# Hybrid decoder step: the last quarter of the out-projection as seven block products, and two pieces of expert weights asked for later

## The chip, the cores and the metric

The kernel runs on one core of one Trainium2 chip. The metric is the device time of one execution in microseconds (us). Three runs of the kernel before gave a median of 1177.78 us (1176.58 to 1179.69).

## What is computed

One layer of a decoder for 320 token rows (256 of a prompt, 64 of eight samples), all in float32. What matters here is what comes after attention:

```
h = x + mixed @ w_out                     # (320, 2048) @ (2048, 2048): the out-projection
n = rms_norm(h, g_ffn)
g_logits = n @ w_rg                       # 4 expert groups, top-1
e_logits = n @ w_re                       # 8 experts in that group, top-2
act  = silu(n @ w_gate[e]) * (n @ w_up[e]) * gates[e]
out  = h + sum over e of act @ w_down[e]  # 32 experts, 256 wide each
```

## The kernel before

Each engine has its own instruction list, written out by hand, and semaphores join them. Four stages follow one another: the projection of the memory tokens, nine chunks of 512 columns of the input projection with the attentions woven between them, the out-projection in four chunks of 512 columns, and the experts.

**A chunk of a projection** takes four quarters of the contraction (`q` = 0 to 3, 512 deep each). A quarter's weights are one block of 1 MB, loaded by SP into one of three slots of `wring` (`weights`). For each quarter PE does three units, and each unit raises `unit_done` by one. There are two ways to do the 256 prompt rows. The plain way is `unit` twice, for 128 rows by 512 columns each (line 576). The other is Winograd's form of Strassen's product: the 256 by 512 deep by 512 columns are seen as two by two blocks, and seven block products of 128 by 256 (line 594) replace eight. `plain_products` does the three whose weights are blocks as loaded, `mixed_products` the four whose weights are sums or differences of blocks. DVE makes those four in `wmix` (`mix_weights`, lines 1292 to 1308) and has made the sums of the tokens before, in `y_mix` (`mix_tokens`). When the last quarter is through, ACT copies the first product out of PSUM (`first_product`), and DVE adds the seven together in `fresh` (`add_products`, lines 1319 to 1323, and `add_fourth`, line 1330). The 64 sample rows are a unit of their own in both ways (`small_unit`, line 586). In the kernel before, chunks 0, 1 and 2 of the out-projection go as seven products and chunk 3 the plain way.

**Behind each chunk of the out-projection** come the residual (lines 1630 and 1634 on DVE; line 1643 for chunk 3), the squares for the norm (line 1205 on ACT), the scaling by `g_ffn` (`scale_tile`, line 1613), the transposes of the 320 rows on PE (`turn_n2`, line 922), their copies out of PSUM on ACT (`turned_n2`, line 1211) and the router's products (`route_sums`, line 930). For chunks 0 to 2 PE does `turn_n2` and `route_sums` inside the next chunk. For chunk 3 they come at the end.

**Routing** goes from the router's logits (copied by ACT, line 1226) through PE transposes and some 40 small DVE operations to a one-hot table, the gather of the first block of tokens (`gather`, line 990) and the list of blocks (`blocks_ready`, line 1733). PE does products with the unit matrix between them (`keep_busy`, line 975), whose results nobody reads.

**The experts** run in blocks of up to 32 tokens of one expert. Each block uses three pieces of weights of 2 MB, two of gate and up, one of down. A ring of eight places (`A_R`, `RING`) takes them. SP asks for pieces 0, 1 and 2 during chunk 0 of the out-projection, since their places are free by then. For piece 7 it waits for `blocks_ready`, and from piece 8 on each place is asked for again when PE is through with what was in it (`piece_used`). Place 3 lies on `A_KV`, where `y_mix` is, and places 4 and 5 lie on `wring` and `wmix`.

Of the kernel before, what the change touches and what calls it, by code (L numbers as in the profile page):

```python
# [24 lines left out]
ALU = mybir.AluOpType  # L25
# [4 lines left out]
P = 128  # L30
# [5 lines left out]
ROWS = [(0, 128), (128, 128), (256, 64)]  # L36
# [7 lines left out]
COLS = 512  # L44
QTR = 4
# [8 lines left out]
UNITS_M, UNITS_X = 4 * QTR, NCHUNK * QTR * 3  # L54
# [65 lines left out]
def hybrid_step(nc, x_rows, mem_rows, x_t, mem_t, w_proj, w_o, kc, vc, mkc, mvc, cst_d, gv_d, gffn_d,  # L120
                relb_d, onehot_d, w_gu, w_dn, mst_d, o_y, o_k, o_v, o_va, o_mk, o_mv,
                bias_d, bias_q_d):
    with ExitStack() as ctx:
# [13 lines left out]
        ps = ctx.enter_context(nc.psum_tensor("ps", [P, 8, 512], F32))  # L137
# [46 lines left out]
        yT = area(A_Y, KT, NT)  # L184
# [43 lines left out]
        hres = area(A_H, 3, D)  # L228
# [81 lines left out]
        unit_done, z_ready = sem("unit_done"), sem("z_ready")  # L310
# [21 lines left out]
        x_again, h_ready = sem("x_again"), sem("h_ready")  # L332
# [35 lines left out]
            return v[:, :, 0, 0:HALF], v[:, :, 0, HALF:COLS], v[:, :, 1, 0:HALF], v[:, :, 1, HALF:COLS]  # L368

        def regions(v):  # L370
            r = 6 if v in (0, 11) else 0
            return r, r + 1, r + 2, 14, r + 3, r + 4, r + 5

        block = ctx.enter_context(nc.Block())
# [3 lines left out]
        def _(sp):  # L378
# [82 lines left out]
            for s in range(UNITS_X):  # L461
# [14 lines left out]
                n, i = sample_step(s)  # L476
# [35 lines left out]
            def piece(u, e):  # L512

                if u % 3 < 2:
                    h = KT // 2 * (u % 3)
                    sp.dma_start(gate_up[u % RING], w_gu[e, :, h:h + KT // 2]).then_inc(ring_loaded[u % RING], 16)
                else:
                    sp.dma_start(down[u % RING], w_dn[e]).then_inc(ring_loaded[u % RING], 16)

            for o in range(1, 13):  # L520
                sp.wait_ge(unit_done, UNITS_M + UNITS_X + 3 * (o + 1))
                weights(47 + o)
                if o in (1, 3, 5):
                    piece(o // 2, 0)
                if o == 11:
                    piece(3, 1)
            sp.wait_ge(unit_done, UNITS_M + UNITS_X + 45)
            piece(4, 1)
            sp.wait_ge(unit_done, UNITS_M + UNITS_X + 48)
            piece(5, 1)  # L530
            piece(6, 2)
            sp.wait_ge(blocks_ready, 1)
# [2 lines left out]
            last = sp.value_load(cnt_i[0:1, 0:1], min_val=NEXP // BODY - 1, max_val=NBLK // BODY - 1)  # L535
# [32 lines left out]
        def _(pe):  # L568
            mm, tr = nc.tensor.matmul, nc.tensor.transpose
            def unit(i, bank, t, src, kq, first, final):  # L570

                pe.wait_ge(w_loaded[i % SLOTS_W], w_count(i))
                r0, m = ROWS[t]
                for k in range(K4):
                    kt = kq * K4 + k
                    last = mm(ps[:, bank + t, :], src[:, kt, r0:r0 + m], wring[:, i % SLOTS_W, k, :],  # L576
                              start=first and k == 0, stop=final and k == K4 - 1)
                last.then_inc(unit_done, 1)

            def small_unit(i, bank, col, src, kq, first, final):  # L580

                pe.wait_ge(w_loaded[i % SLOTS_W], w_count(i))
                for k in range(K4):
                    kt = kq * K4 + k
                    for j in range(2):
                        last = mm(ps[64 * j:64 * j + 64, bank, col:col + HALF], src[:, kt, NPROMPT:NT],  # L586
                                  wring[:, i % SLOTS_W, k, HALF * j:HALF * j + HALF],
                                  start=first and k == 0 and bank != 7, stop=final and k == K4 - 1, skip_group_check=bank == 7)
                last.then_inc(unit_done, 1)
# [326 lines left out]
            def turn_n2(ch, t):  # L916

                r0, m = ROWS[t]
                pe.wait_ge(g_ready, 3 * ch + t + 1)
                for k in range(4):  # L920
                    kt = 4 * ch + k
                    last = tr(ps[:, 3 * (ch % 2) + t, k * 128:k * 128 + m], n2[0:m, t, kt * 128:(kt + 1) * 128], ident[0:m, 0:m])
                last.then_inc(n2_tr, 1)
# [9 lines left out]
            def out_chunk(ch):  # L933
                for q in range(QTR):
                    i = 2 * QTR + NCHUNK * QTR + ch * QTR + q
                    kq = (q + 1) % QTR if ch == 0 else q
                    if ch == 0 and q == QTR - 1:
                        pe.wait_ge(gate_y, G)
                    if ch == 0:
                        pe.wait_ge(y_mixed, q + 1)  # L940
                    for t in range(3):
                        if ch < 3 and t == 0:
                            plain_products(i, 10 + ch, yT, kq, y_mix, q == 0, q == QTR - 1)
                        elif ch < 3 and t == 1:
                            mixed_products(i, 10 + ch, yT, kq, y_mix, q == 0, q == QTR - 1)
                        elif ch < 3:
                            small_unit(i, 7, HALF, yT, kq, q == 0, q == QTR - 1)
                        elif t < 2:
                            unit(i, 3, t, yT, kq, q == 0, q == QTR - 1)
                        else:  # L950
                            small_unit(i, 5, 0, yT, kq, q == 0, q == QTR - 1)
                        if ch == 0 and 3 * q + t < G:
                            gate_turn(3 * q + t)
                        if ch == 3 and q == QTR - 1 and t:
                            turn_n2(3, t - 1)
                    if ch and q == 1:
                        for t in range(3):
                            turn_n2(ch - 1, t)
                    if ch and q == 2:
                        route_sums(ch - 1, 0, NT)  # L960
            for ch in range(4):
                out_chunk(ch)
            turn_n2(3, 2)
            route_sums(3, 0, NPROMPT)
            route_sums(3, NPROMPT, NT).then_inc(lgT_mm, 1)
            pe.wait_ge(lgT_ready, 1)
# [89 lines left out]
        def _(act):  # L1056
# [24 lines left out]
            def first_product(v, last_unit, out):  # L1081

                act.wait_ge(unit_done, last_unit)
                r = regions(v)[0]
                copy(out[:, 0:4:3], psum[:, r:r + 1].to_broadcast([P, 2, HALF])).then_inc(first_copied, 1)
# [122 lines left out]
            def turned_n2(ch, t):  # L1208
# [1 line left out]
                act.wait_ge(n2_tr, 3 * ch + t + 1)  # L1210
                copy(n2T[:, ch % 2, :, r0:r0 + m],
                     ps[:, 3 * (ch % 2) + t, :].rearrange("p (k n) -> p k n", k=4)[:, :, 0:m]).then_inc(n2T_ready, 1)
            for ch in range(3):
                first_product(10 + ch, UNITS_M + UNITS_X + 12 * ch + 10, fresh)
                for t in range(3):
                    square(ch, t)
                for t in range(3):
                    turned_n2(ch, t)
# [40 lines left out]
        def _(dve):  # L1259
# [348 lines left out]
            def scale_tile(ch, t):  # L1608

                m = ROWS[t][1]  # L1610
                cols = slice(ch * COLS, (ch + 1) * COLS)
                dve.wait_ge(h_ready, 3 * ch + t + 1)
                V.tensor_tensor(n2[0:m, t, cols], hres[0:m, t, cols], gff[0:m, cols], ALU.mult).then_inc(g_ready, 1)

            for ch in range(3):
                for q in range(QTR):
                    i = 2 * QTR + NCHUNK * QTR + ch * QTR + q
                    if ch == 0 and q == 2:
                        dve.wait_ge(gate_y, G)
                        mix_tokens(yT, y_mix, 0, y_mixed)  # L1620
                    if q == QTR - 1:
                        add_products(10 + ch, fresh)
                    if ch < 2 or q < QTR - 1:
                        mix_weights(i + 1)
                add_fourth(10 + ch, fresh)
                dve.wait_ge(x_again, 64)
                dve.wait_ge(products_added, 4 * (11 + ch))
                for t in range(2):
                    hh = hres[:, t, ch * COLS:(ch + 1) * COLS]
                    V.tensor_tensor(hh, hh, fresh[:, 2 * t:2 * t + 2].rearrange("p a n -> p (a n)"), ALU.add).then_inc(h_ready, 1)  # L1630
                dve.wait_ge(unit_done, UNITS_M + UNITS_X + 12 * ch + 12)
                for j in range(2):
                    hh = hres[0:64, 2, ch * COLS + HALF * j:ch * COLS + HALF * j + HALF]
                    last = V.tensor_tensor(hh, ps[64 * j:64 * j + 64, 7, HALF:COLS], hh, ALU.add)
                last.then_inc(h_ready, 1)
                for t in range(3):
                    scale_tile(ch, t)
            for t, (_, m) in enumerate(ROWS):
                dve.wait_ge(unit_done, UNITS_M + UNITS_X + 36 + 9 + t + 1)
                for j in range(P // m):  # L1640
                    w = COLS * m // P
                    hh = hres[0:m, t, 3 * COLS + w * j:3 * COLS + w * j + w]
                    last = V.tensor_tensor(hh, ps[m * j:m * j + m, 3 + t, 0:w], hh, ALU.add)
                last.then_inc(h_ready, 1)
                scale_tile(3, t)
            dve.wait_ge(sumsq, 5 + 12)
            link(V.tensor_reduce(st_h, st_hq.rearrange("p (c t) -> p t c", t=3), X, ALU.add))
            V.tensor_scalar(st_h, st_h, 1.0 / D, EPS, ALU.mult, ALU.add).then_inc(ms_ready, 1)
# [313 lines left out]
```

## Time and profile before

| | |
|---|---|
| median of three runs | 1177.78 us (1176.58 to 1179.69) |
| the profiled execution's own time | 1175.47 us |
| span in the trace | 1173.6 us |
| PE busy | 1065.0 us (91%) |
| DVE busy | 533.5 us (45%) |
| ACT busy | 212.4 us (18%) |
| moved by DMA | 385.48 MB, mean 328 GB/s |
| mean granted clock of PE | 0.977 |

The span runs from the first to the last instruction; the execution's own time is 1.9 us longer. Busy time is that of instructions alone, and an engine's idle time matters only where others wait for it. A row of the timeline gives the start in us from the span's start, the time taken, the engine, the line, the operation, and in brackets how long the engine stood idle before and what ended that.

### The profile page before, as it was taken

Reading aid. Unit: us, or ns where it says so; the run is one execution under the profiler, and the core shown is the slowest. Engines: PE = TensorE matmul, PEld = TensorE weight load, DVE = VectorE, ACT = ScalarE, POOL = GpSimd, SP = SyncE. Lnnn points to the kernel's source line nnn. Section 1 sums busy time; section 2 is a strip of 40 time slices with the busy share of each in tenths; the row PEclk is TensorE's granted clock in tenths of the full one; section 3 lists DMA queues with packets and bytes.
Section 4 is the critical chain, followed back from the end, with each engine's and each line's share of the span. In section 5 each row is a group of like instructions: output and inputs, shape, how many; then the busy total and the mean of one; then the engine's idle time right before and its main releaser. Section 6 shows DMA issues by size and latency. Waiting matters only on the chain.

```text
span 1173.6 us, 17462 instructions
## 1 busy us (share of the span) xinstructions
PE 1065.0 (91%) x7153; PEld 589.3 (50%) x7153; DVE 533.5 (45%) x1046; ACT 212.4 (18%) x465; POOL 42.4 (4%) x38
## 2 busy tenths in 40 slices
PE   8998999999999999999999999988788888887885
PEld 3676776665666666677777543323232323232221
DVE  3673555455644565483634244433333333333323
ACT  1111112231212221411001132111111111111110
POOL 0030110001100000010000000000000000000000
PEclk9999999999999999999999999999999999999898
DMA  9989248988999989733953357999999999999994
GB/s 331 351 231 376 81 149 334 336 339 320 360 409 393 378 319 359 295 149 115 371 193 132 144 215 307 424 427 427 428 427 429 428 428 427 428 426 426 427 425 175
DMA packets 38752, 385.48 MB, mean 328 GB/s; under 512 B 4880, under 2 KB 7568, under 8 KB 10224
## 3 DMA queue, kind: packets, MB, share of 16 engines
q1 hardware_dynamic: 36112, 376.87, 80.2%
q0 software_dynamic: 1568, 5.62, 1.8%
q10 hardware_dynamic: 1008, 2.10, 0.5%
q8 instruction: 46, 0.75, 0.3%
q14 instruction: 18, 0.14, 0.0%
HBM read 376.67 MB, written 7.90 MB: 328 GB/s over the span
## 4 chain that ended last, share of the span: by engine, by line
PE 67%; DMA 21%; DVE 5%; issue 2%; ACT 2%; POOL 1%; DVEq 0%; SPq 0%; ACTq 0%; POOLq 0%
PE ps L594 22%; DMA arena<-w_gu 15%; PE ps L586 7%; PE ps L1037 5%; PE ps L1007 5%; PE ps L990 4%; DMA arena<-w_proj 4%; PE ps L788 4%; PE ps L1021 3%; PE ps L755 3%; PE ps L576 3%; DMA arena<-w_dn 3%; PE ps L1014 1%; PE ps L1042 1%; POOL stat L1799 1%
## 5 line engine op out<-in xcount | busy, mean ns | idle before, releaser
L594 PE MATMUL ps<-arena 128*128 128x256 f32 x1456 | 337.2, 386 | 8.1 <-DMA arena<-w_proj 5.3
L594 PEld LDWEIGHTS ps<-arena 128*128 128x128 f32 x1456 | 273.0, 192 | 60.4 <-issue 15.1
L1007 PE MATMUL ps<-arena,cst 128*32 128x512 f32 x1024 | 126.5, 627 | 43.0 <-DMA arena<-w_gu 42.0
L1750 DVE STREAM_TRANSPOSE cst<-ps 128x512 f32<-128x512 f32 x31 | 22.2, 717 | 192.6 <-PE ps L990 192.6
L586 PE MATMUL ps<-arena 128*64 128x256 f32 x832 | 101.3, 385 | 0.0
L1007 PEld LDWEIGHTS ps<-arena,cst 128*32 128x32 f32 x1024 | 32.4, 113 | 130.9 <-issue 86.2
L990 PE MATMUL ps<-arena 128*32 128x512 f32 (+1 forms) x768 | 95.4, 610 | 0.0
L1021 PE MATMUL ps<-arena,cst 128*32 128x512 f32 x512 | 67.3, 646 | 21.4 <-DVE cst L1752 20.1
L586 PEld LDWEIGHTS ps<-arena 128*64 128x64 f32 x832 | 55.1, 136 | 37.8 <-issue 14.1
L1768 DVE COPY arena<-ps 32x512 f32<-32x512 f32 x64 | 44.2, 691 | 51.9 <-PE ps L1021 50.9
L1037 PE MATMUL ps<-arena 128*128 128x512 f32 x128 | 57.0, 598 | 9.6 <-ACT arena L1252 9.6
L1292 DVE TENSOR_TENSOR arena<-arena 128x512 f32<-128x512 f32 x52 | 35.7, 686 | 59.4 <-PE ps L594 42.0
L990 PEld LDWEIGHTS ps<-arena 128*32 128x32 f32 (+1 forms) x768 | 22.8, 113 | 71.3 <-issue 71.3
L1244 ACT COPY arena<-ps 128x512 f32<-128x512 f32 x32 | 18.7, 585 | 195.0 <-PE ps L1007 194.9
L1775 DVE TENSOR_TENSOR arena<-ps,arena 128x512 f32<-128x512 f32 x64 | 44.3, 691 | 21.3 <-PE ps L1037 21.3
L1249 ACT COPY arena<-ps 32x512 f32<-32x512 f32 x64 | 36.8, 574 | 83.2 <-PE ps L1021 82.4
L576 PE MATMUL ps<-arena 128*128 128x512 f32 x112 | 49.6, 597 | 0.2 <-DMA arena<-w_proj 0.2
L788 PE MATMUL ps<-arena 128*32 128x256 f32 (+1 forms) x704 | 45.5, 393 | 4.0 <-ACT arena L1152 4.0
L1799 POOL TENSOR_TENSOR stat<-stat,nhalf 128x24 f32<-128x24 f32 (+4 forms) x9 | 27.6, 3062 | 535.7 <-DVE stat L1382 341.0
L1014 PEld LDWEIGHTS ps<-gv,arena 128*128 128x128 f32 x256 | 31.0, 191 | 27.6 <-issue 26.0
L1037 PEld LDWEIGHTS ps<-arena 128*128 128x128 f32 x128 | 23.7, 190 | 37.5 <-issue 26.8
L755 PE MATMUL ps<-arena 128*32 128x512 f32 (+1 forms) x384 | 39.3, 527 | 2.9 <-DVE arena L1458 2.2
(262 smaller groups left out, 974.6 us busy)
## 6 DMA issues: line engine op xcount, KB each, us to landing
arena<-w_gu SPq DMA_DIRECT2D x64, 2048.0 KB, 33.5
arena<-w_dn SPq DMA_DIRECT2D x32, 2048.0 KB, 31.3
arena<-w_proj SPq DMA_DIRECT2D x43, 1024.0 KB, 7.8
arena<-kc SPq DMA_DIRECT2D x16, 2048.0 KB, 9.3
arena<-vc SPq DMA_DIRECT2D x16, 2048.0 KB, 8.7
arena<-w_o SPq DMA_DIRECT2D x16, 1024.0 KB, 4.9
arena<-kc SPq DMA_DIRECT2D x8, 1024.0 KB, 8.4
arena<-vc SPq DMA_DIRECT2D x8, 1024.0 KB, 10.0
```

The lines of the kernel that those rows point to most:

```text
L576: last = mm(ps[:, bank + t, :], src[:, kt, r0:r0 + m], wring[:, i % SLOTS_W, k, :], start=first and k == 0, stop=final and k == K4 - 1)
L586: last = mm(ps[64 * j:64 * j + 64, bank, col:col + HALF], src[:, kt, NPROMPT:NT], wring[:, i % SLOTS_W, k, HALF * j:HALF * j + HALF], star ...
L594: last = mm(psum[:, regions(v)[j - 1]], left[a], right[:, a], start=first and opens and a == 0, stop=final and a == 1, skip_group_check=True)
L755: last = mm(ps[32 * g:32 * g + 32, 6, 0:w], qpad[:, e * 128 + 32 * g:e * 128 + 32 * g + 32], kp[j][:, e, :], start=half == 0, stop=half == 1)
L788: last = mm(ps[32 * g:32 * g + 32, 5, 0:256], pt_s[0:w, t, 32 * g:32 * g + 32], v, start=t == 0, stop=t == VT)
L990: last = mm(ps[32 * j:32 * j + 32, 1, :], pm[0:m, t, 32 * s:32 * s + 32], n2[0:m, t, 512 * j:512 * j + 512], start=t == 0, stop=t == 2)
L1007: last = mm(ps[g:g + 32, 0, :], xgT[:, s % 2, kt, :], gate_up[(3 * s + h) % RING][:, k, :], start=kt < 4, stop=kt >= KT - 4)
L1014: last = mm(ps[:, 2, 32 * f:32 * f + 32], part[:, 128 * f:128 * f + 128], sel, start=True, stop=True)
L1021: last = mm(ps[32 * g:32 * g + 32, 3, :], actT[:, j, :], down[(3 * s + 2) % RING][:, j, 512 * g:512 * g + 512], start=j == 0, stop=j == 1)
L1037: mm(ps[:, 4 + n, :], pwT[:, t * P:(t + 1) * P], y4[:, 512 * n:512 * n + 512], start=True, stop=True).then_inc(comb_mm, 1)
L1768: V.tensor_copy(y4[32 * b:32 * b + 32, 512 * g:512 * g + 512], ps[32 * g:32 * g + 32, 3, :]).then_inc(ye_copied, 1)
L1775: V.tensor_tensor(hh, ps[:, 4 + n, :], hh, ALU.add).then_inc(added[t], 1)
```

## The change

Chunk 3 of the out-projection is done as chunks 0 to 2 are. PE's loops lose their second branch, and the transposes of chunk 3 come after the whole chunk. DVE mixes the weights of chunk 3 too, and adds its seven products. ACT copies its first product. The products of chunk 3 lie in the banks that chunk 1 used (`regions`, value 13). Since `y_mix` is now read until the chunk's end, SP asks for piece 3 no longer during chunk 3 but behind it. The request for piece 4, which waited for unit 45 of 48, is behind it as well. Pieces 3, 4, 5 and 6 are then asked for in one row, when unit 48 is done.

```diff
         def regions(v):
-            r = 6 if v in (0, 11) else 0
+            r = 6 if v in (0, 11, 13) else 0
...
                 if o in (1, 3, 5):
                     piece(o // 2, 0)
-                if o == 11:
-                    piece(3, 1)
-            sp.wait_ge(unit_done, UNITS_M + UNITS_X + 45)
+            sp.wait_ge(unit_done, UNITS_M + UNITS_X + 48)
+            piece(3, 1)
             piece(4, 1)
-            sp.wait_ge(unit_done, UNITS_M + UNITS_X + 48)
             piece(5, 1)
             piece(6, 2)
...
-                        if ch < 3 and t == 0:
+                        if t == 0:
                             plain_products(i, 10 + ch, yT, kq, y_mix, q == 0, q == QTR - 1)
-                        elif ch < 3 and t == 1:
+                        elif t == 1:
                             mixed_products(i, 10 + ch, yT, kq, y_mix, q == 0, q == QTR - 1)
-                        elif ch < 3:
+                        else:
                             small_unit(i, 7, HALF, yT, kq, q == 0, q == QTR - 1)
-                        elif t < 2:
-                            unit(i, 3, t, yT, kq, q == 0, q == QTR - 1)
-                        else:
-                            small_unit(i, 5, 0, yT, kq, q == 0, q == QTR - 1)
...
-                        if ch == 3 and q == QTR - 1 and t:
-                            turn_n2(3, t - 1)
...
-            turn_n2(3, 2)
+            for t in range(3):
+                turn_n2(3, t)
             route_sums(3, 0, NPROMPT)
...
-            for ch in range(3):
+            for ch in range(4):
                 first_product(10 + ch, UNITS_M + UNITS_X + 12 * ch + 10, fresh)
+                if ch == 3:
+                    break
...
-            for ch in range(3):
+            for ch in range(4):
...
-                    if ch < 2 or q < QTR - 1:
+                    if ch < 3 or q < QTR - 1:
                         mix_weights(i + 1)
...
-            for t, (_, m) in enumerate(ROWS):
-                dve.wait_ge(unit_done, UNITS_M + UNITS_X + 36 + 9 + t + 1)
-                for j in range(P // m):
-                    w = COLS * m // P
-                    hh = hres[0:m, t, 3 * COLS + w * j:3 * COLS + w * j + w]
-                    last = V.tensor_tensor(hh, ps[m * j:m * j + m, 3 + t, 0:w], hh, ALU.add)
-                last.then_inc(h_ready, 1)
-                scale_tile(3, t)
```

On PE, from the last quarter of chunk 3 to the router's products, the order before is this (576: plain product, 586: sample rows, 922: transposes, 930: router):

```order
L576 MATMUL ps<-arena 128x512 x8
L922 MATMUL ps<-cst,arena 128x128 x4
L586 MATMUL ps<-arena 64x256 x8
L922 MATMUL ps<-cst,arena 128x128 x4
L922 MATMUL ps<-cst,arena 128x64 x4
L930 MATMUL ps<-arena,cst 36x256 x4
L930 MATMUL ps<-arena,cst 36x64 x4
```

After the change it is this at the same place (592: block products, 584: sample rows, 920: transposes, 928: router):

```order
L592 MATMUL ps<-arena 128x256 x14
L584 MATMUL ps<-arena 64x256 x8
L920 MATMUL ps<-cst,arena 128x128 x8
L920 MATMUL ps<-cst,arena 128x64 x4
L928 MATMUL ps<-arena,cst 36x256 x4
L928 MATMUL ps<-arena,cst 36x64 x4
```

The first transposes, which stood ahead of the last sample rows, now stand behind them with the others.

On DVE, behind the last mixed weights, the order before is this (1630 and 1634: residual of chunk 2; 1643: residual of chunk 3; 1613: scaling):

```order
L1630 TENSOR_TENSOR arena<-arena 128x512 x2
L1634 TENSOR_TENSOR arena<-ps,arena 64x256 x2
L1613 TENSOR_TENSOR arena<-arena 128x512 x2
L1613 TENSOR_TENSOR arena<-arena 64x512
L1643 TENSOR_TENSOR arena<-ps,arena 128x512
L1613 TENSOR_TENSOR arena<-arena 128x512
L1643 TENSOR_TENSOR arena<-ps,arena 128x512
L1613 TENSOR_TENSOR arena<-arena 128x512
L1643 TENSOR_TENSOR arena<-ps,arena 64x256 x2
L1613 TENSOR_TENSOR arena<-arena 64x512
```

After the change chunk 3 ends on DVE as follows (1314 to 1325: sums of products; 1625 and 1629: residual; 1608: scaling):

```order
L1314 TENSOR_TENSOR arena<-arena,ps 128x2x256
L1316 TENSOR_TENSOR arena<-arena,ps 128x512
L1318 TENSOR_TENSOR arena<-arena,ps 128x2x256
L1325 TENSOR_TENSOR arena<-arena,ps 128x256
L1625 TENSOR_TENSOR arena<-arena 128x512 x2
L1629 TENSOR_TENSOR arena<-ps,arena 64x256 x2
L1608 TENSOR_TENSOR arena<-arena 128x512 x2
L1608 TENSOR_TENSOR arena<-arena 64x512
```

Tile by tile before, residual and scaling now go through all three tiles one after the other, behind the sums of the products.

## Rows read from the trace of the kernel before

**Rows 1.** The page, shares of the chain that ended last, by line.

```profile
PE ps L594 22%; DMA arena<-w_gu 15%; PE ps L586 7%; PE ps L1037 5%; PE ps L1007 5%; PE ps L990 4%; DMA arena<-w_proj 4%; PE ps L788 4%; PE ps L1021 3%; PE ps L755 3%; PE ps L576 3%; DMA arena<-w_dn 3%; PE ps L1014 1%; PE ps L1042 1%; POOL stat L1799 1%
```

**Rows 2.** Windows: length, busy PE PEld DVE ACT POOL, granted clock, DMA share, GB/s.

```profile
700.00:704.00 4.00, 4.00 (x12) 1.04 (x15) 3.76 (x12) 1.32 (x2) 0.00 (x0) 0.58 0.25 107
704.00:708.00 4.00, 3.01 (x28) 0.57 (x24) 2.81 (x14) 0.00 (x0) 0.00 (x0) 1.00 0.00 0
708.00:712.00 4.00, 4.00 (x44) 1.22 (x36) 3.20 (x11) 2.47 (x4) 0.00 (x0) 1.00 0.03 8
712.00:716.00 4.00, 3.35 (x32) 1.42 (x28) 0.94 (x2) 1.11 (x2) 0.00 (x0) 1.00 0.99 360
720.00:1150.00 430.00, 359.90 (x2597) 120.73 (x2589) 150.18 (x241) 66.83 (x131) 0.00 (x0) 0.96 1.01 427
```

**Rows 3.** The page, DMA issues: count, size of each, median us to landing.

```profile
arena<-w_gu SPq DMA_DIRECT2D x64, 2048.0 KB, 33.5
```

**Rows 4.** Timeline of SP's queue, requests for pieces 3 to 7.

```profile
650.10 0.43 SPq L516 DMA_DIRECT2D arena<-w_gu  x1
...
677.97 0.33 SPq L516 DMA_DIRECT2D arena<-w_gu  x1
689.50 0.33 SPq L518 DMA_DIRECT2D arena<-w_dn  x1
689.87 21.48 SPq L516 DMA_DIRECT2D arena<-w_gu  x2
```

**Rows 5.** Timeline, PE: chunk 2 begins, chunk 3 begins, chunk 3 ends.

```profile
613.59 6.31 PE L594 MATMUL ps<-arena 128*128 128x256 f32 x28
...
649.62 7.13 PE L576 MATMUL ps<-arena 128*128 128x512 f32 x16
...
686.98 0.60 PE L922 MATMUL ps<-cst,arena 128*128 128x128 f32 x4
...
687.51 1.95 PE L586 MATMUL ps<-arena 128*64 128x256 f32 x16
```

**Rows 6.** Timeline, DVE behind the last product of chunk 2.

```profile
649.81 0.42 DVE L1330 TENSOR_TENSOR arena<-arena,ps 128x256 f32<-128x256 f32 x1 [0.62 <-PE ps L586]
650.34 1.29 DVE L1630 TENSOR_TENSOR arena<-arena 128x512 f32<-128x512 f32 x2
651.55 0.85 DVE L1634 TENSOR_TENSOR arena<-ps,arena 64x256 f32<-64x256 f32 x2
652.32 1.88 DVE L1613 TENSOR_TENSOR arena<-arena 128x512 f32<-128x512 f32 x3
```

**Rows 7.** Timeline, ACT and PE behind chunk 3: copies, squares, router's products, router's copy.

```profile
687.62 0.58 ACT L1211 COPY arena<-ps 128x512 f32<-128x512 f32 x1 [2.42 <-PE ps L922]
...
688.10 0.63 ACT L1205 ACTIVATE arena<-arena 128x512 f32<-128x512 f32 x1
688.63 0.19 ACT L1205 ACTIVATION_READ_ACCUMULATOR arena<-arena 128x1 f32 x1
...
691.52 2.36 PE L930 MATMUL ps<-arena,cst 128*36 128x256 f32 x16
...
693.93 0.42 ACT L1226 COPY arena<-ps 36x320 f32<-36x320 f32 x1 [1.30 <-PE ps L930]
```

**Rows 8.** Timeline, the first gather and the request for piece 7.

```profile
703.27 2.94 PE L990 MATMUL ps<-arena 128*32 128x512 f32 x24
...
711.02 0.33 SPq L516 DMA_DIRECT2D arena<-w_gu  x1
```

**Rows 9.** Timeline, PE: the products with the unit matrix, first and second time.

```profile
694.70 2.84 PE L975 MATMUL ps<-cst 128*128 128x512 f32 x6
...
699.76 3.58 PE L975 MATMUL ps<-cst 128*128 128x512 f32 x4
```

**Rows 10.** Windows with one PE wait for expert weights in each, columns as in rows 2.

```profile
908.50:914.80 6.30, 3.41 (x21) 0.97 (x24) 0.00 (x0) 0.00 (x0) 0.00 (x0) 0.75 1.02 432
1026.20:1032.50 6.30, 3.44 (x32) 0.94 (x32) 0.00 (x0) 0.58 (x1) 0.00 (x0) 1.00 1.01 429
```

## The prediction

> **What bounds the kernel now.** I read the page's chain first: where does the time of the last step come from? Up to the routing it is PE's block products (22% and 7% of the span in two lines), behind it transfers of expert weights (15% and 3%) [rows 1]. The windows say how hard that second bound is: from 720 to 1150 us the DMA engines are busy all the time and move 427 GB/s, while PE works 359.9 of 430 us [rows 2]. The weights set the pace there, and nothing that PE, DVE or ACT gain inside that stretch comes out. So I ask what starts the stretch. SP's queue answers: piece 7 is asked for at 711.02 [rows 8], when the list of blocks is ready. Ahead of it the DMA engines are idle, with shares of 0.00 from 704 to 708 and 0.03 from 708 to 712, and from 712 on they are full [rows 2]. From then on one stream of 2 MB pieces runs to the end. The end therefore moves by as much as the list of blocks moves, if the pieces asked for before it have landed by then. The change touches the last quarter of the out-projection, the chain from it to that list, and the order of four requests; each is costed at that point.
>
> **PE's products in chunk 3.** A quarter of prompt rows takes 28 PE instructions in 6.31 us as block products and 16 in 7.13 us as plain ones [rows 5], so four quarters save 4 x 0.82 = 3.3 us. A check by whole chunks: chunk 2 took 649.62 - 613.59 = 36.03 us with the transposes and router's products of chunk 1 inside, and chunk 3 will now hold the same, so PE's last sample rows end about 36.03 us after 649.62, at 685.65. Before they ended at 687.51 + 1.95 = 689.46 [rows 5]. That is 3.8 us earlier: the 3.3, and the 0.60 of first transposes that now stand behind. The mixed weights for chunk 3 cost DVE nothing on the path: it sat idle in chunk 3, and in chunk 2, where it mixed as much, PE lost no time (36.03 us includes that). If that cover were gone, each quarter could wait on one or two additions of the size in line 1330 or 1630, 0.4 to 0.7 us [rows 6].
>
> **The tail behind it grows.** Before, two of three tiles were through residual, squares and transposes while PE still worked. What remained from 689.46 to the router's copy at 693.93 [rows 5, 7] is 4.5 us. Now all of it follows the last product. DVE shows how long that takes in chunk 2, where the same four steps stand at 649.81 to 652.32 and end 1.88 later, at 654.20 [rows 6]. Shifted by 36.03 us, the sums come at 685.84 and the three scalings from 688.35 to 690.23. The first scaling takes 0.69 or so (three in 1.88, overlapping), so PE transposes from 689.1. ACT copied 687.62 - 686.98 = 0.64 after the start of the transposes [rows 5, 7], so it copies at 689.75. Its next square begins 0.48 later, as it did at 688.10 after 687.62, and occupies it for 0.63 + 0.19 = 0.82 [rows 7]; so the second copy starts at 691.05 and ends at 691.65. The first part of the router's products waits for that copy. Both parts took 2.36 us and the router's copy came 0.05 later [rows 7], so it comes at 691.65 + 2.36 + 0.05 = 694.06, against 693.93: **0.1 us later**. What PE saves, the tail takes. The bounds of this term: if the whole tail hid as it did before, -3.8; if ACT and DVE each slipped by one more small step, +1.
>
> **The clock behind the idle PE.** PE now stands idle from 685.65 to 689.1, and then has only transposes until 691.65. The trace of before has no such place in the routing. Its nearest rows are two waits for expert weights, each in a stretch of 6.30 us in which PE worked 3.4: after one the granted clock was 0.75 on the mean, so part of it at 1.2 GHz in place of 2.4, after the other it stayed at 1.00 [rows 10]. What the low level costs is also there: behind the second ranking, where the clock is 0.58 from 700 to 704 [rows 2], four products with the unit matrix take 3.58 us where six took 2.84 at the full clock [rows 9], 0.90 against 0.47 each. Of the path here it can touch the router's products, 2.36 us, which would double. So the cost lies between 0 and +2.4; since one of the two waits went each way and a fall need not cover all of it, I take +0.8. The Trainium skill, page "TensorE: Matmul & The Clock Gate", section "Why this matters for your kernels", tells to leave no idle gaps of PE between bursts of matmuls, because the clock then goes back to half its rate. By that rule alone the term would be +2.4, by the second wait above 0; rows 10 agree with it once and once not.
>
> **The four requests.** Pieces 3 and 4 went out at 650.10 and 677.97, pieces 5 and 6 at 689.50 and 689.87 [rows 4]. Now all four go when PE ends, from about 685.7, some 0.4 apart. They are 4 x 2048 KB = 8.4 MB [rows 3], or 19.6 us at 427 GB/s; with a start at 687 they have landed by 707. At the slowest rate in these rows, the 360 GB/s of 712 to 716, it is 23.3 us and 710 [rows 2]. Both are ahead of piece 7 at 711. The two moved pieces thus fill a hole in which the DMA engines had nothing to do: cost 0. If that cover were gone, two pieces at 427 GB/s are 9.8 us. PE needs pieces 3 and 4 for the second block, 10 us or more after the gather at 703.27 [rows 8], long after they land. On SP nothing stands behind these requests but that for piece 7, which waits for the list anyway; PE, DVE and ACT wait for none of them earlier than before.
>
> **The sum.** On the path: 0.1 (tail against PE) + 0.8 (clock) + 0 (requests) = +0.9 us. On the profiled execution, 1175.47 us of its own with a span of 1173.6, that is 1176.4. This execution was 2.3 us below the median of the runs shown, so on the median of 1177.78 the forecast is **1178.7 us**: no change that can be told. About 0.3%, or 3.5 us, is what a measurement of this kernel can tell from none.
>
> **The rivals.**
> - *The clock falls and stays* (slower). For it: the new gap of about 3.4 us and a thin stretch behind it. If the low level reaches from the router's products to the first gather, both double: 2.36 + 2.94 [rows 7, 8] = 5.3 us, and with the 0.1 the time is 1183.2. Against it: between the two PE works on products with the unit matrix (2.84 us for six, [rows 9]), and before the clock was back at 1.00 by 704 [rows 2]. It decides once more than 3.4 us of low-clock products lie on the path. The skill's rule named above speaks for this case. Chance 0.08.
> - *The moved pieces are late* (slower). If the stream of four isn't through when piece 7 is asked for, the end moves by what is left, at worst the whole 9.8 us: 1187.7. It would need under 8.4 MB / 25 us = 336 GB/s between 686 and 711. Against it: 427 GB/s wherever the stream is full, 360 even in the stretch where it starts [rows 2]. Chance 0.04.
> - *The tail hides* (faster). If the residual, scaling and copies overlap the last products as before, PE's whole 3.8 us reach the list of blocks: 1174.0. For it: the plain tail did overlap. Against it: a Winograd block is whole only when all seven are added, and rows 6 show DVE doing that behind the last product of chunk 2. Chance 0.05.
>
> **How the numbers follow.** My forecast, an end moved by less than 3.5 us either way, has 0.83, the rivals 0.08, 0.04 and 0.05. So faster by over 0.3% 0.05, within it 0.83, slower 0.12. For the range I take the forecast's own bounds: the sum lies between 0.1 and 2.5 us, and the median of three runs between 1.2 below and 1.9 above, as the runs shown do. That gives 1176.7 to 1182.2; for a tail that hides in part I go 1.2 lower, to 1175.5. It leaves out most of the three rivals, 0.15.
>
> **What would show it.** In the trace after: PE's last sample rows of chunk 3 end near 685.7 and its first transposes behind them start near 689.1; the router's copy on ACT comes between 694 and 696.5; four requests stand in a row on SP from about 685.7; the DMA engines are full from about 687 to 707, idle for a few us, and full again from piece 7 on; piece 7 is asked for between 711 and 714. The prediction is wrong if piece 7 moves by more than 3.5 us, or if the DMA engines don't fall idle ahead of it, so that the two moved pieces add to the stream that ends the kernel, or if the stream from 720 on runs at another rate than 427 GB/s.

## The result and the profile after

The changed kernel took 1180.94 us (median of 22 runs, 1175.84 to 1183.74) against 1176.68 us for the kernel before (22 runs, 1172.22 to 1182.52). The ratio is 1.0031 with a 95% interval of 1.0018 to 1.0044, so 3.6 us slower, 2.1 to 5.2 (the two medians lie 4.3 us apart). The profiled execution took 1178.16 us with a span of 1176.3.

The page's chain has kept its two bounds. Line 592, which now does all four chunks, has 24%, where lines 594 and 576 had 22% and 3% [rows 1].

```profile
PE ps L592 24%; DMA arena<-w_gu 14%; PE ps L584 7%; PE ps L1000 5%; PE ps L1030 5%; DMA arena<-w_proj 4%; PE ps L983 4%; PE ps L786 4%; PE ps L1014 3%; PE ps L753 3%; DMA arena<-w_dn 3%; PE ps L1007 1%; PE ps L1035 1%; POOL stat L1786 1%; PE ps L695 1%
```

Windows of the trace after (length, busy PE PEld DVE ACT POOL, granted clock, DMA share, GB/s). The stream runs at 427 GB/s as before, and the hole in front of piece 7 is there still: the share is 0.02 from 708 to 712 [rows 2]. New is where the clock falls: in the stretch 688 to 692, ahead of the router's sums, and it stays at half, 1.2 GHz in place of 2.4, until past 700. (Before, it was low behind that, 0.58 from 700 to 704 [rows 2].)

```profile
688.00:692.00 4.00, 1.94 (x13) 1.35 (x14) 2.43 (x5) 2.04 (x7) 0.00 (x0) 0.86 1.01 430
692.00:696.00 4.00, 4.00 (x16) 2.10 (x14) 0.60 (x5) 0.56 (x2) 0.88 (x1) 0.50 0.99 422
696.00:700.00 4.00, 3.49 (x9) 1.67 (x8) 2.40 (x22) 3.76 (x3) 0.00 (x0) 0.50 1.03 442
...
704.00:708.00 4.00, 2.81 (x25) 0.65 (x24) 3.76 (x13) 0.00 (x0) 0.00 (x0) 1.00 0.73 311
708.00:712.00 4.00, 3.01 (x29) 0.84 (x28) 3.20 (x13) 0.27 (x2) 0.00 (x0) 1.00 0.02 4
...
720.00:1150.00 430.00, 360.47 (x2601) 120.72 (x2593) 151.01 (x243) 67.42 (x132) 0.00 (x0) 0.96 1.01 427
```

PE's timeline after: chunk 3 begins, its last sample rows (584), the transposes (920), the router's sums (928), the products with the unit matrix (968), the first products of the ranking (971) and the first gather (983).

```profile
649.84 2.42 PE L592 MATMUL ps<-arena 128*128 128x256 f32 x10
...
684.00 1.95 PE L584 MATMUL ps<-arena 128*64 128x256 f32 x16
689.30 1.67 PE L920 MATMUL ps<-cst,arena 128*128 128x128 f32 x12 [3.36 <-DVE arena L1608]
691.73 4.48 PE L928 MATMUL ps<-arena,cst 128*36 128x256 f32 x16 [0.76 <-ACT arena L1204]
...
697.18 4.77 PE L968 MATMUL ps<-cst 128*128 128x512 f32 x6
701.78 0.36 PE L971 MATMUL ps<-arena,cst 128*128 128x96 f32 x2
...
702.37 1.96 PE L968 MATMUL ps<-cst 128*128 128x512 f32 x4
705.52 2.92 PE L983 MATMUL ps<-arena 128*32 128x512 f32 x24 [1.19 <-DVE arena L1686]
```

DVE's end of chunk 3, in the order that rows 6 showed for chunk 2:

```profile
686.06 0.42 DVE L1325 TENSOR_TENSOR arena<-arena,ps 128x256 f32<-128x256 f32 x1 [0.62 <-PE ps L584]
686.58 1.29 DVE L1625 TENSOR_TENSOR arena<-arena 128x512 f32<-128x512 f32 x2
687.79 0.85 DVE L1629 TENSOR_TENSOR arena<-ps,arena 64x256 f32<-64x256 f32 x2
688.57 1.88 DVE L1608 TENSOR_TENSOR arena<-arena 128x512 f32<-128x512 f32 x3
```

SP's queue, pieces 3 to 7:

```profile
685.98 0.80 SPq L516 DMA_DIRECT2D arena<-w_gu  x2
686.83 0.43 SPq L518 DMA_DIRECT2D arena<-w_dn  x1
687.30 26.28 SPq L516 DMA_DIRECT2D arena<-w_gu  x2
```

The last of these rows holds the requests for pieces 6 and 7. A request takes 0.33 [rows 8], so piece 7 is asked for at 687.30 + 26.28 - 0.33 = 713.25. I measure from the start of chunk 3, since the stage before it differs from execution to execution: 711.02 - 649.62 = 61.40 us before [rows 5, 8], 713.25 - 649.84 = 63.41 after. **The list of blocks is 2.0 us later.** PE ends the chunk 36.11 us after its start (684.00 + 1.95 - 649.84) in place of 39.84, 3.7 us earlier; the tail, from there to the request for piece 7, takes 5.7 us more. Of that, 2.1 us is the router's sums: 4.48 us in place of 2.36 [rows 7], at half the clock.

### The profile page after: what moved, and what is told of

It reads as the page before. It is cut to its first block, busy times and chain, and to the rows that moved or that the text cites. A ratio compares the mean times of both kernels' runs of the same rounds, so it can differ in the third digit from the quotient of the medians.

```text
span 1176.3 us, 17595 instructions
## 1 busy us (share of the span) xinstructions
PE 1062.9 (90%) x7201; PEld 598.8 (51%) x7201; DVE 546.0 (46%) x1066; ACT 212.8 (18%) x466; POOL 42.4 (4%) x38
## 4 chain that ended last, share of the span: by engine, by line
PE 67%; DMA 21%; DVE 5%; issue 2%; ACT 2%; POOL 1%; ACTq 0%; DVEq 0%; SPq 0%; POOLq 0%
PE ps L592 24%; DMA arena<-w_gu 14%; PE ps L584 7%; PE ps L1000 5%; PE ps L1030 5%; DMA arena<-w_proj 4%; PE ps L983 4%; PE ps L786 4%; PE ps L1014 3%; PE ps L753 3%; DMA arena<-w_dn 3%; PE ps L1007 1%; PE ps L1035 1%; POOL stat L1786 1%; PE ps L695 1%
## 5 line engine op out<-in xcount | busy, mean ns | idle before, releaser
L592 PE MATMUL ps<-arena 128*128 128x256 f32 x1568 | 362.5, 386 | 9.5 <-DMA arena<-w_proj 6.1
L592 PEld LDWEIGHTS ps<-arena 128*128 128x128 f32 x1568 | 294.0, 192 | 66.6 <-issue 18.2
L983 PE MATMUL ps<-arena 128*32 128x512 f32 (+1 forms) x768 | 95.3, 610 | 1.2 <-DVE arena L1686 1.2
L1287 DVE TENSOR_TENSOR arena<-arena 128x512 f32<-128x512 f32 x56 | 38.4, 686 | 68.3 <-PE ps L592 50.2
L1030 PE MATMUL ps<-arena 128*128 128x512 f32 x128 | 57.0, 598 | 9.9 <-ACT arena L1247 9.9
L1786 POOL TENSOR_TENSOR stat<-stat,nhalf 128x24 f32<-128x24 f32 (+4 forms) x9 | 27.6, 3062 | 535.2 <-DVE stat L1377 339.2
L1007 PEld LDWEIGHTS ps<-gv,arena 128*128 128x128 f32 x256 | 31.0, 191 | 27.6 <-issue 26.0
L1314 DVE TENSOR_TENSOR arena<-arena,ps 128x512 f32<-128x512 f32 x14 | 9.6, 687 | 75.8 <-PE ps L592 72.6
L1030 PEld LDWEIGHTS ps<-arena 128*128 128x128 f32 x128 | 23.7, 190 | 37.8 <-issue 26.8
L1303 DVE TENSOR_TENSOR arena<-arena 128x512 f32<-128x512 f32 x56 | 38.8, 692 | 6.9 <-PE ps L592 1.9
```

The costliest lines, as they stand in the source:

```text
L592: last = mm(psum[:, regions(v)[j - 1]], left[a], right[:, a], start=first and opens and a == 0, stop=final and a == 1, skip_group_check=True)
L983: last = mm(ps[32 * j:32 * j + 32, 1, :], pm[0:m, t, 32 * s:32 * s + 32], n2[0:m, t, 512 * j:512 * j + 512], start=t == 0, stop=t == 2)
L1007: last = mm(ps[:, 2, 32 * f:32 * f + 32], part[:, 128 * f:128 * f + 128], sel, start=True, stop=True)
L1030: mm(ps[:, 4 + n, :], pwT[:, t * P:(t + 1) * P], y4[:, 512 * n:512 * n + 512], start=True, stop=True).then_inc(comb_mm, 1)
L1303: V.tensor_tensor(wmix[:, 3], b21, wmix[:, 1], ALU.subtract).then_inc(w_mixed, 1)
L1786: g.tensor_tensor(out, in_, nhalf[:, 0:in_.shape[1]], ALU.pow).then_inc(rs_ready, 1)
```

## Experiments

Two theories. **A:** the clock falls behind PE's new idle time, and the router's sums run at half rate. **B:** the requests or the longer tail cost the time, whatever the clock. Below, "to piece 7" is the time from the end of the last sample rows of chunk 3 to the request for piece 7: 21.56 us before, 27.30 after. Each experiment is an edit of one of the two kernels; one is the changed kernel once more, as it is. A trace shows one execution, a ratio all of a run's. The first four ran on one chip beside 35 runs of the kernel before, the next four beside another 35, the last three beside 29.

**The requests alone** (`e2_requests`, on the kernel before).

```diff
-                if o == 11:
-                    piece(3, 1)
-            sp.wait_ge(unit_done, UNITS_M + UNITS_X + 45)
-            piece(4, 1)
             sp.wait_ge(unit_done, UNITS_M + UNITS_X + 48)
+            piece(3, 1)
+            piece(4, 1)
             piece(5, 1)
```

> The kernel before, with nothing changed but SP's order: pieces 3 and 4 are asked for when unit 48 is done, ahead of 5 and 6. Theory A: the four pieces land by 711 us (request at 689.5, 19.7 us of stream, so 709 to 711), piece 7 is asked for at 711 as before, and the time is that of the kernel before, within 0.1%. Theory B: the time is 1.002 to 1.004 of the kernel before; if the two pieces were not hidden at all it would be 9.8 us more, 1.008.

Ratio 1.0007 (0.9991 to 1.0023). SP's queue and a window of this run:

```profile
692.43 20.68 SPq L516 DMA_DIRECT2D arena<-w_gu  x2
```

```profile
708.00:712.00 4.00, 3.04 (x30) 0.99 (x34) 3.59 (x12) 0.74 (x2) 0.00 (x0) 1.00 1.02 434
```

To piece 7 it is 21.7 us, and the transfers, which start 3.7 us later against chunk 3 than in the changed kernel, fill the hole to 712 and are through when piece 7 is asked for at 712.78. The order of the requests costs 0.15 us. Theory B's first half falls.

**A fill, too large** (`e1_fill`, on the changed kernel).

Here `fill(n)` does n products of the unit matrix with 512 columns of constants, into a bank that nobody reads:

```diff
+            fill(7)
             for t in range(3):
                 turn_n2(3, t)
+            fill(1)
             route_sums(3, 0, NPROMPT)
```

> The changed kernel with seven products with the unit matrix put on PE between the last product of chunk 3 and its first transposes, and one more ahead of the router's sums; nobody reads them. Theory A (the clock falls behind the idle PE and the router's sums run at half rate): the clock stays at 1.00 from 686 to 696 us, the router's sums take 2.4 us in place of 4.5, piece 7 is asked for about 2.1 us earlier than in the changed kernel, at 711.2 to 711.6, and the time is 2 us or more below the changed kernel's, within 0.1% of the kernel before. Theory B (the two moved requests cost the time, by late landing or contention): the fill changes nothing, the time stays at 1.003 of the kernel before.

Ratio 1.0022 (1.0008 to 1.0036), and to piece 7 27.6 us: no gain. The timeline of PE says why:

```profile
688.20 6.28 PE L958 MATMUL ps<-cst 128*128 128x512 f32 x14
...
696.73 2.36 PE L928 MATMUL ps<-arena,cst 128*36 128x256 f32 x16
```

The clock held and the router's sums took 2.36 us, as theory A has it. The fill itself was twice as long as I had meant: each of these products stands as two rows of the trace, so seven are 14 rows and 6.28 us, and they held the transposes up by 2.7 us. (So the six and four products that the prediction read in rows 9 are three and two.) The expectation of the time missed by my count.

**The fill in its right size** (`e5_fill3`): `fill(3)` ahead of the transposes, and no other.

> The changed kernel with three products with the unit matrix (0.95 us each) between the last product of chunk 3 and the first transposes, where the first fill had seven and held the transposes up. Theory A (the clock falls behind the idle PE): the clock stays at 1.00, the first transposes start 3.4 us behind the last sample rows as in the changed kernel, the router's sums take 2.4 us, and the request for piece 7 comes 25.1 to 25.3 us behind the last sample rows (changed kernel 27.3, kernel before 21.6 with the last sample rows 3.5 us later). The time is then 0.999 to 1.001 of the kernel before. Theory B (the tail or the requests cost the time whatever the clock): 27 us there and 1.002 to 1.003.

Ratio 1.0006 (0.9990 to 1.0022). PE and SP:

```profile
686.92 1.95 PE L584 MATMUL ps<-arena 128*64 128x256 f32 x16
688.80 2.84 PE L958 MATMUL ps<-cst 128*128 128x512 f32 x6
692.23 1.66 PE L920 MATMUL ps<-cst,arena 128*128 128x128 f32 x12 [0.59 <-DVE arena L1613]
694.65 2.36 PE L928 MATMUL ps<-arena,cst 128*36 128x256 f32 x16 [0.76 <-ACT arena L1209]
```

```profile
690.23 24.26 SPq L516 DMA_DIRECT2D arena<-w_gu  x2
```

The transposes start 3.4 us behind the last sample rows and the router's sums 5.8 us, as in the changed kernel; only the clock is different, and the sums take 2.36. Piece 7 is asked for 25.3 us behind the last sample rows, 2.0 less than after the change. That is 25.3 + 36.1 = 61.4 us from the start of chunk 3, the 61.40 of the kernel before. With the clock held, the change costs nothing at this point, and without it 2.0 us: theory A in the trace. The time points the same way, but doesn't show it alone: on the same chip the changed kernel without the fill has 1.0024 (`e7_after`, next), and the two intervals overlap.

**The changed kernel again** (`e7_after`).

> The changed kernel once more, unchanged, for a second trace and beside the others on one chip. Theory A: the router's sums run at half rate in most executions, so in this trace too: 27 us from the last sample rows to the request for piece 7, and the time 1.001 to 1.004 of the kernel before. If this trace has the clock at 1.00 there, 25.2 us.

Ratio 1.0024 (1.0010 to 1.0038), to piece 7 27.2 us. The sums ran at half rate again:

```profile
685.30 26.15 SPq L516 DMA_DIRECT2D arena<-w_gu  x2
687.30 2.09 PE L920 MATMUL ps<-cst,arena 128*128 128x128 f32 x12 [3.36 <-DVE arena L1608]
689.72 4.48 PE L928 MATMUL ps<-arena,cst 128*36 128x256 f32 x16 [0.34 <-ACT arena L1204]
```

In a third trace with this tail (`e10_after_end`, below) they take 4.48 us too. From the start of chunk 3 to piece 7 these three take 63.4, 63.3 and 63.3 us; the three traces with the old tail (before, `e2_requests`, `e9_before_end`) 61.4, 61.6 and 61.4. Nor is the fall one of traced executions alone: the mean granted clock of a whole execution, averaged over the twelve of this run, is 0.971, over the twelve of `e5_fill3` 0.975, and 0.975 for the kernel before beside them.

**Tile by tile** (`e3_tiles`, on the changed kernel): for chunk 3 DVE does the first tile's residual ahead of `add_fourth`, which it doesn't need, and each tile's scaling right behind its residual.

```diff
+                if ch == 3:
+                    dve.wait_ge(products_added, 4 * (10 + ch) + 3)
+                    residual(0)
+                    add_fourth(10 + ch, fresh)
+                    scale_tile(3, 0)
+                    dve.wait_ge(products_added, 4 * (11 + ch))
+                    residual(1)
+                    scale_tile(3, 1)
```

> The changed kernel with DVE's end of chunk 3 done tile by tile: the first tile's residual ahead of the fourth sum, and each tile's scaling right behind its residual. Theory A: transposes of the first tile start near 687.5 in place of 689.3, PE's longest gap falls from 3.4 to about 1.5 us, and the router's sums start near 690.3 in place of 691.7. If the clock holds, they take 2.4 us and the time falls by 3.5 us against the changed kernel, to 0.999 of the kernel before; if the clock falls all the same, by 1.4 us. Theory B: the tail's order doesn't matter beyond 1.4 us.

Ratio 1.0001 (0.9982 to 1.0020), to piece 7 26.2 us.

```profile
689.86 0.66 PE L920 MATMUL ps<-cst,arena 128*128 128x128 f32 x4 [1.28 <-DVE arena L1608]
691.18 0.66 PE L920 MATMUL ps<-cst,arena 128*128 128x128 f32 x4 [0.67 <-DVE arena L1608]
692.67 0.69 PE L920 MATMUL ps<-cst,arena 64*128 64x64 f32 x4 [0.83 <-DVE arena L1608]
693.28 4.48 PE L928 MATMUL ps<-arena,cst 128*36 128x256 f32 x16
```

The longest wait is 1.28 us now, and the clock falls all the same: there are only three waits ahead of and between short transposes. 1.1 us is won at piece 7, against the 1.4 expected if the clock falls. The time doesn't go with that: 1.0001 is 3.5 us below the changed kernel's 1.0031, as was expected for a clock that holds, though the two intervals leave room for 1.1. The trace is of the slowest of the twelve executions (1182.37 us, of 1173.82 to 1182.37), so the clock may have held in others; no run shows that. What is shown is that the clock can fall without a long wait, not that it always does.

**Tiles and fill** (`e4_tiles_fill`: three products ahead of the first transposes, one behind them; `e6_tiles_fill`: one ahead, and half a product of 256 columns behind the first and the second transposes).

> Both: DVE tile by tile, and four products with the unit matrix on PE, three ahead of the first transposes and one behind them. Theory A: the clock stays at 1.00, the router's copy comes near 692.7 (before the change 693.9, with it 696.2), piece 7 is asked for near 709.8, and the time is 1 to 1.5 us below the kernel before, ratio 0.999. Theory B: it stays above the kernel before, at 1.001 to 1.002.

> DVE tile by tile, and PE's gaps filled in the right size: one product with the unit matrix ahead of the first transposes and half a one behind the first and the second. Theory A: the clock stays at 1.00, the router's sums start 4.6 us behind the last sample rows, and piece 7 is asked for 23.7 us behind them (24.3 with the larger fill), which is 1.4 us ahead of the kernel before: ratio 0.998 to 1.000. If the clock falls all the same, 25.8 us and 1.000 to 1.002.

Ratios 0.9999 (0.9981 to 1.0017) and 1.0005 (0.9989 to 1.0020). In the traces both hold the clock and reach piece 7 after 24.3 and 23.6 us; the first one's fill held the first transposes up by 1.3 us. The second one's rows:

```profile
686.25 0.66 PE L920 MATMUL ps<-cst,arena 128*128 128x128 f32 x4 [0.22 <-DVE arena L1616]
686.74 0.60 PE L958 MATMUL ps<-cst 128*128 128x256 f32 x2
...
689.45 2.36 PE L928 MATMUL ps<-arena,cst 128*36 128x256 f32 x16
...
1151.53 3.64 PE L1022 MATMUL ps<-arena,cst 128*32 128x512 f32 x16 [0.65 <-DVE cst L1761]
1155.10 0.99 PE L1030 MATMUL ps<-cst 128*128 128x128 f32 x3
1156.98 8.84 PE L1038 MATMUL ps<-arena 128*128 128x512 f32 x16 [0.89 <-ACT arena L1255]
```

Piece 7 is 1.7 us ahead of the kernel before (23.6 + 36.1 = 59.7 against 61.4), but the time isn't. In this execution the very last block ran at half rate: its down products take 3.64 us (2.95 before, 3.48 after, so the clock was low there too for a part) and the last products of the kernel 8.84, where both the kernel before and the changed one show 7.13. From the request for piece 7 to the end of the span it is 465.8 us in `e3_tiles` and `e6_tiles_fill` and 465.6 in `e4_tiles_fill`, 462.6 before and 463.1 after. That led to the last group.

**Fills in the last block** (`e8_end`: `e6_tiles_fill` with these and a fourth product behind the router; `e11_best`: the same kernel again; `e9_before_end` and `e10_after_end`: these alone, on the kernel before and on the changed one). `end_fill` is `fill` with another bank.

```diff
+                    last_block = final and s == BODY - 1
+                    if last_block:
+                        end_fill(1)
                     for h in range(2):
+                        if last_block and h:
+                            end_fill(2)
                         loaded(i, 3 * s + h)
...
+                    if last_block:
+                        end_fill(1)
                     loaded(i, 3 * s + 2)
...
                     last.then_inc(pwt_mm, 1)
+                    if last_block:
+                        end_fill(1)
```

> As the run with tiles and right-sized fills, and the same remedy at two more places where PE waits: a fourth product with the unit matrix behind the router, and such products in the very last expert block (one and two while it waits for its two pieces of gate and up, one ahead of the piece of down, one behind the transposes). Theory A carried on: what differs from run to run at the end is the clock in the last block, so the stretch from the request for piece 7 to the end of the span, 462.1 to 465.8 us in the traces so far, is at or below 462.1, and the time is 0.996 to 0.998 of the kernel before. If the end isn't set by the clock, that stretch stays between 462 and 466 and the time is 0.999.

> The kernel before with products with the unit matrix in the last expert block alone, so that the clock holds to the end. Theory A (the end differs from run to run by the clock): the stretch from the request for piece 7 to the end of the span falls to 462 us or less, and the time is 0.998 to 0.9995 of the kernel before, with a smaller spread. If it isn't the clock, the time is that of the kernel before.

> The changed kernel with the same products in the last block. Beside the run with these products in the kernel before it gives what the change costs without the end's own differences. Theory A (the change costs what its half-rate router's sums put on the path, 1.9 us in the two traces, and nothing at the end): the median is 1.5 to 2.5 us above that run's. If the change also makes the end slower, by where the clock falls in the last block, these products take that part away, and the rest of the 3.6 us measured for the change shows here as less than 2 us. If the difference stays at 3 us or more, something between the routing and the end is dearer than the traces show.

> The run with tiles, fills, a fourth product behind the router and the products in the last block, once more, beside the two others. Theory A: 23.6 us from the last sample rows to the request for piece 7, no more than 462 us from there to the end, a median 1.5 to 2.5 us below the kernel before with products in the last block alone, and a ratio of 0.997 to 0.999 to the kernel before.

| run | median us | ratio to before (95%) | to piece 7, us | piece 7 to end, us |
|---|---|---|---|---|
| `e8_end` | 1175.38 | 0.9985 (0.9973 to 0.9997) | 23.6 | 461.8 |
| `e9_before_end` | 1174.74 | 0.9976 (0.9959 to 0.9993) | 21.6 | 461.9 |
| `e10_after_end` | 1179.24 | 1.0011 (0.9990 to 1.0033) | 27.2 | 463.4 |
| `e11_best` | 1175.60 | 0.9976 (0.9954 to 0.9998) | 23.6 | 463.5 |

The end of `e9_before_end`, where the clock held, and of `e11_best`, where it fell for a while all the same:

```profile
1158.49 1.92 PE L1033 MATMUL ps<-arena,cst 128*32 128x512 f32 x16
...
1162.23 7.13 PE L1051 MATMUL ps<-arena 128*128 128x512 f32 x16 [0.19 <-ACT arena L1266]
```

```profile
1156.78 2.76 PE L1034 MATMUL ps<-arena,cst 128*32 128x512 f32 x16
1159.47 0.64 PE L1042 MATMUL ps<-cst 128*128 128x128 f32 x3
1160.04 1.13 PE L1002 MATMUL ps<-cst 128*128 128x512 f32 x2
1161.37 7.13 PE L1052 MATMUL ps<-arena 128*128 128x512 f32 x16 [0.20 <-ACT arena L1269]
```

Three of the four lie below the kernel before with their whole intervals: `e9_before_end` and `e11_best` by 0.24% and `e8_end`, the same kernel as `e11_best`, by 0.15%. They share the fills in the last block, and `e9_before_end` has nothing else, so those carry its gain; the mean granted clock of its twelve executions is 0.978, against 0.975 for the kernel before beside it. What the better tail adds, 1.7 us at piece 7 in the traces, doesn't show between these two medians, and no run here separates it. The expectation that `e11_best` would be 1.5 to 2.5 us below `e9_before_end` missed; so did that of 462 us at its end. In `e8_end` and `e9_before_end` the end came as expected, with ratios a little beside the 0.996 to 0.998 and 0.998 to 0.9995 expected. `e10_after_end` lies 4.5 us above `e9_before_end` where 1.5 to 2.5 were expected, with intervals of some 2 us on each. From 3 us on, the expectation said, something behind the routing is dearer than the traces had shown. In these two traces it is the end: the change costs 1.9 us at piece 7 and 1.5 behind it, where the clock fell in the last block of `e10_after_end` and not in that of `e9_before_end`. Whether the change brings that about or the execution, no run settles.

## Why the prediction came out as it did

It forecast +0.9 us and no change that can be told. Measured is +3.6 us, 0.31%, just over the 3.5 us that the prediction took for the least that can be told. The time, 1180.94 us, is inside the stated range, but in part by luck: the change lies above the 0.1 to 2.5 us that the prediction gave its sum, and the base of 1177.78 us from three runs was 1.1 us above the median of 22. The 2.0 us at piece 7 lie inside the sum's bounds. The steps:

- **What sets the end.** Held. From piece 7 on the stream runs at 427 GB/s in both traces, and the end follows the list of blocks.
- **PE in chunk 3.** 3.8 us earlier predicted, 3.7 measured.
- **The tail.** Predicted to take that back, with 0.1 left. The first transposes came at 689.30 (predicted 689.1), the router's sums at 691.73 (691.65). With the clock held the balance at piece 7 is 0.0 us (`e5_fill3`). Reading chunk 2's tail for chunk 3's was right.
- **The requests.** Cost 0 predicted, 0.15 measured alone (`e2_requests`); the four pieces had landed by 708 and the DMA engines idled to 712 in the trace after.
- **The clock.** This is the step that failed, by its size: "since one of the two waits went each way and a fall need not cover all of it, I take +0.8". The sums ran at half rate in each of three traces with this tail, and the term is 4.48 - 2.36 = 2.1 us, near the upper bound of 2.4. The waits of rows 10 were poor stand-ins, as I read it: behind each of them PE went on with products without a gap, while here the idle time is followed by short transposes. The trace of `e3_tiles` shows that in such a stretch the clock can fall with no wait over 1.28 us; that the transposes make the difference to rows 10 isn't shown. The rule of the Trainium skill that the prediction weighed (page "TensorE: Matmul & The Clock Gate", section "Why this matters for your kernels") was the better guide, and its +2.4 was nearly what came.
- **The first rival**, the clock low as far as the first gather, came half true. The clock stayed low past 700, and the products with the unit matrix took 4.77 us for 2.84 [rows 9], but that cost nothing more at piece 7. It held the first products of the ranking up by about half a microsecond, to 701.78. The second group of products with the unit matrix then ran at the full clock, 1.96 us in place of the 3.58 [rows 9] behind which the gather had waited before, and gave it back. From the router's copy to piece 7 it is 17.0 us, as it was before (17.1). The gather ran at full rate (2.92 us, [rows 8]: 2.94).

So 2.0 of the 3.6 us are shown in the traces and put down to the clock by `e5_fill3`. The rest isn't settled. From piece 7 to the end, three traces with the old tail (before, `e2_requests`, and `e9_before_end` with its fills at the end) have 462.6, 463.5 and 461.9 us, three with the changed tail (after, `e7_after`, and `e10_after_end` with the same fills) 463.1, 464.4 and 463.4. That is 1.0 us more on the mean, but the two groups overlap, `e1_fill` and `e5_fill3` lie among them (462.1, 463.3), and the start of chunk 3 alone lies anywhere between 649.6 and 654.6 us in the first three. The interval of 2.1 to 5.2 us would nearly admit the 2.0 alone.

## What to carry to other kernels

A faster step in front of a serial tail pays only if what overlapped it before can still overlap it: here seven products that are whole only at the end lengthened the tail by the 3.7 us that PE had won, and nothing was left. Look next at what the shorter step does to the engine that then waits, since its clock may fall just where its work is on the path; a few idle products that fit the waits held it here, and their length must be read from the trace. The two transfers moved into a hole in front of the stream that sets the end cost next to nothing (0.15 us), since they landed inside the hole.

## What was not expected of the hardware

In one traced execution the clock fell in a stretch without any long wait (1.28, 0.67 and 0.83 us, ahead of and between transposes of 0.66 us, `e3_tiles`) and stayed at half for the next products, while half a product of 0.60 us in each of two waits, and one of 1.13 ahead of them, held it in another (`e6_tiles_fill`). The end of the kernel, which no one had touched, takes 461.8 to 465.8 us from piece 7 on by where and how long the clock is low in the last block; with products put into its waits, the clock held there in two of four traces, and they are at the bottom of that (461.8, 461.9; the other two 463.4 and 463.5).
